# Half of the MLP up-projections of two stages as pairs of 64-row matmuls in two row halves of the array

## The chip, the cores and the metric

One NeuronCore of a Trainium2 chip runs the whole program. The metric is the device time of one execution in microseconds. The kernel before was timed in three runs, and one execution of it was recorded by the profiler.

## The reference

Three transformer blocks follow one another on one sequence of 1024 tokens with 1024 features, all in float32. Each block has a mixer (gated delta rule and neighbourhood attention in the first, sliding-window attention and a convolution in the second, gated linear attention and a convolution in the third) and an MLP. The change touches only the MLPs of block 1 and block 3. In block 1 it is

```python
x = layer_norm(DEEPNORM_ALPHA * x + mix, ln1_g[l], ln1_b[l])
ff = jnp.square(jax.nn.relu(jnp.einsum('btd,df->btf', x, w1[l]) + b1[l]))
ff = jnp.einsum('btf,fd->btd', ff, w2[l]) + b2[l]
```

with 4096 hidden features. The MLP of block 3 is the same without the biases, after an RMS norm.

## The kernel before

**Data.** Activations are stored with features on the partitions and tokens along the free dimension. The 1024 tokens are two halves of 512. A float32 product is made of three matmuls on operands of type fp32r (a float32 rounded to fewer mantissa bits): each activation and each weight is split into a high and a low part, and the three passes are high by high, low activation by high weight and high activation by low weight (`passes`, L283).

**Units.** The work of TensorE is a list `order` of units. One unit uses 128x1024 weights, which SyncE loads into one of four slots (`load_sp`, L270). ScalarE makes `w_hi` (`split_act`, L275) and VectorE makes `w_lo` (`split_dve`, L280) two units ahead of use. The MLP of one half is 64 units: 32 of kind "up" and 32 of kind "down". An up unit makes 128 of the hidden features for 512 tokens: 8 contracted chunks of 128 rows by 3 passes, 24 matmuls of 128x512 into one PSUM bank (`unit_part`, L341). A down unit also has 24 matmuls, 12 into each of two banks (L319), and it contracts four hidden chunks.

**Order.** An MLP half runs five up units, then four down, four up, four down and so on in eight groups: the first up unit of the next group stands ahead of the down units of a group, so the four chunks that a group of down units reads are ready one unit early. Only in the last group do the down units come directly behind the last up unit.

**Eviction of an up unit.** ScalarE applies Relu from PSUM into `u_act` (L373), which frees the bank, squares it into `h_hi` (L375) and again in place (L376). VectorE subtracts to get `h_lo` (L386). A down unit is added to the residual by VectorE (L402), and so is a unit of kind "out", the output projection (L408). Background units use two pairs of banks in turn, so a unit needs the pair that the unit before the last one used.

**Order by hand.** All engines walk the same list of steps (`walk`). A step may carry pieces of other work ("segments"), and on each engine those come first, then the weight split for the unit two places on, then the unit's own eviction. Each engine's queue is strictly in order. In the first half of MLP 1, the layer norm of the other half is laid beside units 0, 2, 4, ... 14 (`ln_dve`: sum L549, centring L555, squares folded L484 to L496, scaling L510, `low` L567 and L569). In the second half of MLP 3 the final RMS norm of the first half is laid beside units 2 to 8 (L484 to L500, L510). In both stages no other background runs.

Of the kernel before, what the change touches and what calls it, by code (L numbers as in the profile page):

```python
# [10 lines left out]
ALU = mybir.AluOpType  # L11
ACT = mybir.ActivationFunctionType
AX = mybir.AxisListType

P = 128
D = 1024
DC = D // P
T = 1024
HALF = 512
TC = T // P  # L20
# [103 lines left out]
def build_program(nc, g):  # L124

    ctx = ExitStack()
    with ctx:
# [16 lines left out]
        def sem(name):  # L144
            return ctx.enter_context(nc.semaphore(name))

        def param(name, j=0, n=1):
            return params[:, bass.ds(j + PARAMS[name][0], n)]
# [29 lines left out]
        def acts(h, low, c, t0=META, t1=W):  # L178
            return acts1[:, low, c, t0 - META:t1 - META] if h else acts0[:, low, c, t0:t1]
# [10 lines left out]
        u_act = mlp.take("u_act", [P, 2, HALF])  # L190
        out_at = mlp.at

        ps = ctx.enter_context(nc.psum_tensor("ps", [P, 8, HALF], F32))
# [4 lines left out]
        def tokens(h, t=None):  # L198
            t = xT if t is None else t
            return t[:, :, h * HALF:(h + 1) * HALF]  # L200
# [24 lines left out]
                self.ks, self.back, self.whole, self.taken = range(DC), None, kind in WHOLE, 0  # L225


        early1, last_down = [], []
        WHOLE = ("ab1", "cv1", "z1", "nq1", "nk1")
        NV = 4  # L230
        order = []
# [22 lines left out]
        def unit_done(eng, u):  # L254
            if u.src is None:
                eng.wait_ge(side_done, u.side + 1)
            else:
                eng.wait_ge(mm_done[u.z], u.turn + 1)

        def bank_free(u):  # L260
            return free[u.pool][u.slot]

        def own_free(eng, u):
            eng.wait_ge(bank_free(u), u.use + 1)
# [18 lines left out]
        def passes(z):  # L283

            return (w_hi[z], 0), (w_hi[z], 1), (w_lo[z], 0)
# [40 lines left out]
        def unit_part(pe, u, first, stop):  # L326

            if first == 0 and u.taken:
                if u.use:
                    pe.wait_ge(bank_free(u), u.use)  # L330
                pe.wait_ge(w_split[u.z], u.turn + 1)
            for h in range(2) if u.whole else [u.half]:
                spans = [(0, W // 2), (W // 2, W)] if u.meta else [(META, W)]
                for i_k in range(first, stop):
                    k = u.ks[i_k]
                    if u.gate is not None:
                        u.gate(pe, h, i_k)
                    for i, (w, low) in enumerate(passes(u.z)):
                        for b, (t0, t1) in enumerate(spans):
                            bank = u.bank + (h if u.whole else b)  # L340
                            last = nc.tensor.matmul(ps[:, bank, 0:t1 - t0], w[:, k * P:(k + 1) * P], acts(h, low, k, t0, t1),  # L341
                                                    start=(i_k == 0 and i == 0), stop=(i_k == DC - 1 and i == 2))
            if stop == DC:
                last.then_inc(mm_done[u.z], 1)
# [11 lines left out]
        def unit_act(act, u):  # L356
            if u.kind in ("out", "down"):
                return
            if u.kind == "nv1":
                if u.j == NV - 1:  # L360
                    nv1_act(act)
                return
            if u.kind in EVICT_ACT:
                unit_done(act, u)
                EVICT_ACT[u.kind](act, u)
                return
            if u.kind == "up":
                s = u.chunk % 2
                unit_done(act, u)
                if u.chunk >= 2:  # L370
                    act.wait_ge(hid_ready, u.chunk - 1)
                bias = param("b1", 4 * u.gr + u.j) if u.bias else 0.0
                nc.scalar.activation(u_act[:, s, :], ps[:, u.bank, :], ACT.Relu, bias=bias).then_inc(bank_free(u), 1)  # L373
                own_free(act, u)
                nc.scalar.activation(h_hi[:, u.chunk % RING, :], u_act[:, s, :], ACT.Square)  # L375
                nc.scalar.activation(u_act[:, s, :], u_act[:, s, :], ACT.Square).then_inc(hid_hi, 1)  # L376

        def unit_dve(dve, u):
            if u.kind == "nv1" and u.j == NV - 1:
                nv1_dve(dve)  # L380
            if u.kind in EVICT_DVE:
                EVICT_DVE[u.kind](dve, u)
            if u.kind == "up":
                r = u.chunk % RING
                dve.wait_ge(hid_hi, u.chunk + 1)
                nc.vector.tensor_tensor(h_lo[:, r, :], u_act[:, u.chunk % 2, :], h_hi[:, r, :].bitcast(F32), ALU.subtract)\  # L386
                    .then_inc(hid_ready, 1)
            if u in last_down:
                for c in range(2):
                    if c:  # L390
                        unit_done(dve, u)
                    else:
                        dve.wait_ge(tail_tile, 1)
                    one = tokens(u.half)[:, 2 * u.j + c, :]
                    nc.vector.tensor_tensor(one, one, ps[:, u.bank + c, :], ALU.add).then_inc(bank_free(u) if c else tail_added, 1)
                    if c == 0:
                        last_fold_dve(dve, rms_final[1])
                return
            if u.kind == "down":
                unit_done(dve, u)  # L400
                two = tokens(u.half)[:, 2 * u.j:2 * u.j + 2, :]
                nc.vector.tensor_tensor(two, two, ps[:, u.bank:u.bank + 2, :], ALU.add).then_inc(bank_free(u), 1)  # L402
            if u.kind == "out":
                unit_done(dve, u)
                if u.back is not None:
                    dve.wait_ge(u.back, 48)
                one = xT[:, u.j, u.half * HALF:(u.half + 1) * HALF]
                nc.vector.tensor_tensor(one, one, ps[:, u.bank, :], ALU.add).then_inc(bank_free(u), 1)  # L408
# [272 lines left out]
        def last_fold_dve(dve, m):  # L681
            m.wait(dve, "pre", 2)
            nc.vector.tensor_tensor(m.q[:, 0, :], m.q[:, 0, :], m.q[:, 1, :], ALU.add).then_inc(m.s["pre"], 1)
# [149 lines left out]
        def nv1_act(act):  # L833
            for at, b in enumerate(NV_LAST):
                if at < TC - 1:
                    act.wait_ge(nv_pe, at + 1)
                else:
                    unit_done(act, nv1s[-1])
                nc.scalar.activation(n_v[:, b, :], ps[:, b, :], ACT.Copy).then_inc(nv_act, 1)
                if at == 4:  # L840
                    for d in range(2):
                        identity_act(act, d)

        def nv1_dve(dve):
            for d in range(2):
                decayed_dve(dve, 0, d)
                for piece in first_level(dve, 0, d):
                    pass
# [345 lines left out]
        go = {name: sem(f"go_{name}") for name in ["sq", "sum", "ln", "rs", "norm", "end"]}  # L1194
# [1376 lines left out]
        gl = {name: old for name, (old, _) in zip(gl_names, gl_old)}  # L2571
        gl0 = {name: count for name, (_, count) in zip(gl_names, gl_old)}

        def gla_pool(pool):

            pool.wait_ge(sa["end"], sa0["end"] + 2 * HB)
            pool.wait_ge(c_tap, 2 * CC * CK)
            nc.gpsimd.dma_start(metaT[:, :, :], g["meta"]).then_inc(l_in, 16)
            nc.gpsimd.dma_start(l_wg[:, :], g["w_gate"]).then_inc(l_in, 16)
            nc.gpsimd.dma_start(l_mask[:, :, :], g["gla_consts"]).then_inc(l_in, 16)  # L2580
# [575 lines left out]
        mlp1 = [mlp_half("w_mlp1", h, True) for h in range(2)]  # L3156
        mlp2 = [mlp_half("w_mlp2", h) for h in range(2)]
        mlp3 = [mlp_half("w_mlp3", h) for h in range(2)]
# [135 lines left out]
        one = [(u, ()) for u in proj1]  # L3294
# [19 lines left out]
        last = [(u, ()) for u in mlp3[1]]  # L3314
# [7 lines left out]
        for m in (mlp1, mlp2, mlp3):  # L3322
            for h in range(2):
                chunk0 = m[h][0].chunk
                for u in m[h]:
                    if u.kind == "down":
                        u.first = chunk0 + 4 * u.gr
        early1.extend(proj1[:2])
        FIRST1 = len(proj1)
        AHEAD = 2  # L3330

# [23 lines left out]
        def _(sp):  # L3355
# [13 lines left out]
            for u in proj1:  # L3369
                if u.n + SLOTS < FIRST1:  # L3370
                    load_sp(sp, order[u.n + SLOTS])
# [12 lines left out]
            sp.wait_ge(na["av"], NP * ROWS)  # L3384
            for u in order[FIRST1:FIRST1 + SLOTS]:
                if u.z == 0:
# [3 lines left out]
            residual_sp(sp, 1)  # L3390
            for u in order[FIRST1 + SLOTS:]:
                load_sp(sp, u)
# [18 lines left out]
        def _(act):  # L3411
            act.preload_act_table_set(LOG_EXP)
            front_act(act)
            walk(act, front, "act", unit_act, split_act, 0, FIRST1)
            end1_act(act)
            walk(act, rest, "act", unit_act, split_act, FIRST1)

        @block.vector
        def _(dve):
# [3 lines left out]
            front_dve(dve)  # L3423
            walk(dve, front, "dve", unit_dve, split_dve, 0, FIRST1)
            end1_dve(dve)
# [146 lines left out]
```

## Time and profile before

| | us |
|---|---|
| three timed runs | 3663.24 median (3659.82 to 3664.07) |
| the profiled execution, its own time | 3661.55 |
| span of its trace | 3659.4 |
| TensorE matmuls busy | 3598.4 (98%) |
| VectorE busy | 2144.2 (59%) |
| ScalarE busy | 1579.6 (43%) |
| granted clock of TensorE, mean share of full speed | 0.995 |

The profiled execution took 2.2 us more than its span, which is what lies outside the first and the last instruction. The two stages that the change touches are the first half of MLP 1 (784.7 to 1135.2 us of the span) and the second half of MLP 3 (3298.1 to 3646.7 us), and TensorE is busy all through both of them.

### The profile page before, as it was taken

To read this page: it belongs to the slowest core of one execution; us is meant where nothing else is said; L and a number is where in the kernel's file an instruction comes from. 1 tells how busy PE (TensorE), PEld (TensorE's weight loads), DVE (VectorE), ACT (ScalarE), POOL (GpSimd) and SP (SyncE) were. 2 spreads that over 40 slices of the span, in tenths; PEclk is the share of its full clock that TensorE was granted. 3 is DMA by queue.
4 is the path that set the end of the run, shared out by engine and by line. 5 is a ranking of instruction groups with operands and counts; after the bars stand their busy time and mean duration, and the time that the engine had idled before them with its cause. 6 is when DMAs were issued, how large, how long until landed. Compare 5 with 4: busy or idle time off the path is not lost.

```text
span 3659.4 us, 50653 instructions
## 1 busy us (share of the span) xinstructions
PE 3598.4 (98%) x21121; PEld 2959.4 (81%) x21121; DVE 2144.2 (59%) x3262; ACT 1579.6 (43%) x2544; POOL 81.4 (2%) x85
## 2 busy tenths in 40 slices
PE   8999899999999999999999999999999999999998
PEld 5888778788888878888888889888888888888887
DVE  5741687775345578757588564366655266555333
ACT  5451666644334444535344452333443333434333
POOL 0000121000000000000000000000000000000000
PEclk9999899999999999999999999999999999999999
DMA  5124321324322222222222322222222222223222
GB/s 202 47 72 113 78 68 51 119 92 115 106 97 98 96 84 78 96 97 93 90 78 93 98 88 91 93 81 87 86 94 97 93 87 81 84 95 121 98 98 87
DMA packets 118891, 340.27 MB, mean 93 GB/s; under 512 B 20089, under 2 KB 32393, under 8 KB 118537
## 3 DMA queue, kind: packets, MB, share of 16 engines
q1 hardware_dynamic: 116424, 331.52, 28.0%
q0 software_dynamic: 2240, 5.51, 0.7%
q8 instruction: 169, 2.77, 0.3%
q14 instruction: 58, 0.47, 0.0%
HBM read 318.47 MB, written 20.06 MB: 93 GB/s over the span
## 4 chain that ended last, share of the span: by engine, by line
PE 94%; DVE 4%; ACT 1%; issue 1%; DMA 0%; SPq 0%; ACTq 0%; DVEq 0%
PE ps L341 54%; PE ps L319 28%; PE ps L1337 1%; PE ps L821 1%; PE ps L2847 1%; PE ps L1045 1%; PE ps L1693 1%; PE ps L1660 1%; DVE n_s L1782 1%; PE ps L1348 1%; PE ps L2276 0%; DVE g_D L1524 0%; PE ps L2303 0%; PE ps L1670 0%; PE ps L1380 0%
## 5 line engine op out<-in xcount | busy, mean ns | idle before, releaser
L341 PE MATMUL ps<-acts,w_hi 128*128 128x512 f32 (+1 forms) x6064 | 1813.1, 383 | 2.5 <-ACT l_vf L2683 0.8
L341 PEld LDWEIGHTS ps<-acts,w_hi 128*128 128x128 f32 x6064 | 1110.2, 188 | 231.9 <-issue 10.6
L341 PE MATMUL ps<-acts,w_lo 128*128 128x512 f32 (+1 forms) x3032 | 1136.1, 381 | 0.0
L280 DVE TENSOR_TENSOR w_lo<-w_raw,w_hi 128x1024 fp32r<-128x1024 f32 x539 | 657.8, 1221 | 390.9 <-ACT w_hi L275 387.9
L275 ACT ACTIVATE w_hi<-w_raw 128x1024 fp32r<-128x1024 f32 x539 | 563.6, 1050 | 500.3 <-DMA w_raw<-in_w_mlp 316.5
L341 PEld LDWEIGHTS ps<-acts,w_lo 128*128 128x128 f32 x3032 | 561.5, 188 | 110.0
L319 PE MATMUL ps<-h_hi,w_hi 128*128 128x512 f32 x1528 | 478.0, 394 | 0.0
L319 PE MATMUL ps<-h_lo,w_hi 128*128 128x512 f32 x1528 | 471.1, 390 | 0.0
L319 PE MATMUL ps<-h_hi,w_lo 128*128 128x512 f32 x1528 | 470.9, 389 | 0.0
L386 DVE TENSOR_TENSOR h_lo<-u_act,h_hi 128x512 fp32r<-128x512 f32 x192 | 132.8, 692 | 436.4 <-ACT u_act L376 435.9
L402 DVE TENSOR_TENSOR xT<-xT,ps 128x1024 f32<-128x1024 f32 x191 | 232.8, 1219 | 235.1 <-PE ps L319 234.4
L319 PEld LDWEIGHTS ps<-h_hi,w_lo 128*128 128x128 f32 x1528 | 286.8, 188 | 60.4
L319 PEld LDWEIGHTS ps<-h_lo,w_hi 128*128 128x128 f32 x1528 | 286.8, 188 | 60.3
L319 PEld LDWEIGHTS ps<-h_hi,w_hi 128*128 128x128 f32 x1528 | 283.6, 188 | 62.3 <-issue 4.4
L373 ACT ACTIVATE u_act<-ps 128x512 f32<-128x512 f32 x128 | 76.4, 596 | 336.6 <-PE ps L341 336.6
L2247 DVE SCALAR_TENSOR_TENSOR mixh<-c_pad,params,mixh 128x512 f32<-128x512 f32 x240 | 163.6, 744 | 0.0
L373 ACT ACTIVATE u_act<-ps,params 128x512 f32<-128x512 f32 x64 | 44.0, 688 | 191.1 <-PE ps L341 191.1
L375 ACT ACTIVATE h_hi<-u_act 128x512 fp32r<-128x512 f32 x192 | 121.4, 632 | 6.1
L376 ACT ACTIVATE u_act<-u_act 128x512 f32<-128x512 f32 x192 | 118.2, 616 | 0.0
L408 DVE TENSOR_TENSOR xT<-xT,ps 128x512 f32<-128x512 f32 x48 | 32.9, 686 | 123.8 <-PE ps L341 123.8
L2909 ACT ACTIVATE l_e<-l_e 128x256 f32<-128x256 f32 x56 | 23.4, 418 | 139.9 <-DVE l_e L2945 138.9
L476 ACT ACTIVATE acts<-mixh 128x512 fp32r<-128x512 f32 x64 | 40.5, 633 | 78.3 <-DVE mixh L510 77.2
(392 smaller groups left out, 2944.0 us busy)
## 6 DMA issues: line engine op xcount, KB each, us to landing
w_raw<-in_w_mlp SPq DMA_DIRECT2D x384, 512.0 KB, 3.4
w_raw<-in_w_in SPq DMA_DIRECT2D x107, 512.0 KB, 3.4
w_raw<-in_w_out SPq DMA_DIRECT2D x48, 512.0 KB, 3.4
n_bias<-na_tab SPq DMA_DIRECT2D x36, 256.0 KB, 4.6
xT<-in_x SPq DMA_DIRECT2D x8, 512.0 KB, 8.2
x<-xT SPq DMA_DIRECT2D x2, 2048.0 KB, 8.2
g_row<-gate_rows SPq DMA_DIRECT2D x16, 256.0 KB, 3.4
xT<-x SPq DMA_DIRECT2D x2, 2048.0 KB, 12.4
```

Of the source, the lines that this page charges most:

```text
L275: nc.scalar.activation(w_hi[u.z][:, :], w_raw[u.z][:, :], ACT.Copy).then_inc(w_hi_done[u.z], 1)
L280: nc.vector.tensor_tensor(w_lo[u.z][:, :], w_raw[u.z][:, :], w_hi[u.z][:, :].bitcast(F32), ALU.subtract).then_inc(w_split[u.z], 1)
L319: last = nc.tensor.matmul(ps[:, u.bank + c, :], w[:, k * 256 + c * P:k * 256 + (c + 1) * P], act[:, (u.first + k) % RING, :], start=(k == ...
L341: last = nc.tensor.matmul(ps[:, bank, 0:t1 - t0], w[:, k * P:(k + 1) * P], acts(h, low, k, t0, t1), start=(i_k == 0 and i == 0), stop=(i_k ...
L373: nc.scalar.activation(u_act[:, s, :], ps[:, u.bank, :], ACT.Relu, bias=bias).then_inc(bank_free(u), 1)
L375: nc.scalar.activation(h_hi[:, u.chunk % RING, :], u_act[:, s, :], ACT.Square)
L376: nc.scalar.activation(u_act[:, s, :], u_act[:, s, :], ACT.Square).then_inc(hid_hi, 1)
L386: nc.vector.tensor_tensor(h_lo[:, r, :], u_act[:, u.chunk % 2, :], h_hi[:, r, :].bitcast(F32), ALU.subtract)\
L402: nc.vector.tensor_tensor(two, two, ps[:, u.bank:u.bank + 2, :], ALU.add).then_inc(bank_free(u), 1)
L476: nc.scalar.activation(acts(m.half, 0, c), src, ACT.Copy).then_inc(m.s["hi"], 1)
L821: last = nc.tensor.matmul(ps[:, b, :], acts(b // HB, low, 2 * u.j + k, t0, t0 + P), w[:, k * HALF:(k + 1) * HALF], start=(u.j == 0 and k = ...
L2247: nc.vector.scalar_tensor_tensor(y, x, w, y, op0=ALU.mult, op1=ALU.add).then_inc(c_tap, 1)
```

## The change

The 64 up units of these two half-MLPs form the list `by_rows`. Each of their 24 matmuls of 128 contracted rows becomes two of 64 rows: partitions 0 to 63 go to one half of the array's rows and accumulate into bank `u.bank`, partitions 64 to 127 go to the other half and accumulate into `u.bank + 1`. The two banks must then be added. ScalarE copies the second bank into `u_act`, VectorE adds the first bank onto it and frees both, ScalarE applies Relu with the bias in place, waits for its own write, and goes on with the two squares as before. `rows_copied` and `rows_relu` are semaphores of an earlier stage, counted on from there.

```diff
@@ unit_part @@
                     for i, (w, low) in enumerate(passes(u.z)):
+                        if u in by_rows:
+                            for b in range(2):
+                                rows = slice(P // 2 * b, P // 2 * b + P // 2)
+                                last = nc.tensor.matmul(ps[:, u.bank + b, :], w[rows, k * P:(k + 1) * P], acts(h, low, k)[rows],
+                                                        start=(i_k == 0 and i == 0), stop=(i_k == DC - 1 and i == 2))
+                            continue
@@ unit_act @@
-                nc.scalar.activation(u_act[:, s, :], ps[:, u.bank, :], ACT.Relu, bias=bias).then_inc(bank_free(u), 1)
-                own_free(act, u)
+                if u in by_rows:
+                    n = by_rows.index(u)
+                    nc.scalar.activation(u_act[:, s, :], ps[:, u.bank + 1, :], ACT.Copy).then_inc(rows_copied, 1)
+                    own_free(act, u)
+                    nc.scalar.activation(u_act[:, s, :], u_act[:, s, :], ACT.Relu, bias=bias).then_inc(rows_relu, 1)
+                    act.wait_ge(rows_relu, TC + n + 1)
+                else:
+                    nc.scalar.activation(u_act[:, s, :], ps[:, u.bank, :], ACT.Relu, bias=bias).then_inc(bank_free(u), 1)
+                    own_free(act, u)
@@ unit_dve @@
+            if u in by_rows:
+                dve.wait_ge(rows_copied, TC + by_rows.index(u) + 1)
+                one = u_act[:, u.chunk % 2, :]
+                nc.vector.tensor_tensor(one, one, ps[:, u.bank, :], ALU.add).then_inc(bank_free(u), 1)
             if u.kind == "up":
@@ after the units are placed @@
+        by_rows.extend(u for u in mlp1[0] + mlp3[1] if u.kind == "up")
```

## Rows read from the trace of the kernel before

**Rows 1.** The page: span, busy time of the engines, and the chain by engine.

```profile
span 3659.4 us, 50653 instructions
PE 3598.4 (98%) x21121; PEld 2959.4 (81%) x21121; DVE 2144.2 (59%) x3262; ACT 1579.6 (43%) x2544; POOL 81.4 (2%) x85
...
PE 94%; DVE 4%; ACT 1%; issue 1%; DMA 0%; SPq 0%; ACTq 0%; DVEq 0%
```

**Rows 2.** Windows over the two stages: length, busy us of each engine, clock, DMA.

```profile
784.70:1135.19 350.49, 350.49 (x1544) 288.87 (x1543) 170.25 (x172) 133.58 (x173) 9.21 (x16) 1.00 0.35 104
3298.06:3646.68 348.62, 348.62 (x1540) 288.67 (x1539) 151.45 (x148) 129.90 (x171) 4.34 (x8) 1.00 0.30 98
```

**Rows 3.** Timeline of PE: first matmuls of four up units and of those behind.

```profile
3478.04 0.61 PE L341 MATMUL ps<-acts,w_hi 128*128 128x512 f32 x2
...
3499.80 0.61 PE L319 MATMUL ps<-h_hi,w_hi 128*128 128x512 f32 x2
```

**Rows 4.** PE: pairs of 64-row matmuls, full float32 ones; then one group (busy, mean).

```profile
1341.38 0.61 PE L319 MATMUL ps<-h_hi,w_lo 128*128 128x512 f32 x2
1341.92 2.00 PE L2303 MATMUL ps<-s_k,s_q 64*128 64x256 f32 x16
1343.85 0.74 PE L319 MATMUL ps<-h_hi,w_hi 128*128 128x512 f32 x2
...
1344.90 0.40 PE L319 MATMUL ps<-h_hi,w_lo 128*128 128x512 f32 x1
...
2420.25 1.13 PE L2864 MATMUL ps<-l_vt,l_ket 128*128 128x256 f32 x4
...
L1045 PE MATMUL ps<-norm_b,consts 128*128 128x512 f32 x22 | 9.9, 597 | 2.4 <-ACT norm_b L1095 2.4
```

**Rows 5.** Timeline, one up unit's eviction and the matmuls that follow it.

```profile
3586.84 0.61 PE L319 MATMUL ps<-h_hi,w_hi 128*128 128x512 f32 x2
...
3587.03 0.60 ACT L373 ACTIVATE u_act<-ps 128x512 f32<-128x512 f32 x1 [2.71 <-PE ps L341]
...
3587.66 0.63 ACT L375 ACTIVATE h_hi<-u_act 128x512 fp32r<-128x512 f32 x1
...
3588.20 0.62 ACT L376 ACTIVATE u_act<-u_act 128x512 f32<-128x512 f32 x1
...
3588.72 1.04 ACT L275 ACTIVATE w_hi<-w_raw 128x1024 fp32r<-128x1024 f32 x1
3588.85 0.69 DVE L386 TENSOR_TENSOR h_lo<-u_act,h_hi 128x512 fp32r<-128x512 f32 x1 [3.27 <-ACT u_act L376]
```

**Rows 6.** Timeline of DVE and ACT at the start of MLP 1's first half.

```profile
789.27 0.69 DVE L408 TENSOR_TENSOR xT<-xT,ps 128x512 f32<-128x512 f32 x1
790.06 2.29 DVE L549 TENSOR_TENSOR mixh<-xT 128x2048 f32<-128x2048 f32 x1
790.23 0.69 ACT L373 ACTIVATE u_act<-ps,params 128x512 f32<-128x512 f32 x1 [6.35 <-PE ps L341]
...
795.39 0.69 DVE L386 TENSOR_TENSOR h_lo<-u_act,h_hi 128x512 fp32r<-128x512 f32 x1
...
798.30 4.48 DVE L555 SCALAR_TENSOR_TENSOR xT<-ps,xT 128x2048 f32<-128x2048 f32 x2
802.70 1.22 DVE L280 TENSOR_TENSOR w_lo<-w_raw,w_hi 128x1024 fp32r<-128x1024 f32 x1
```

**Rows 7.** Timeline of DVE at units 12 to 14 of that stage.

```profile
854.06 2.73 DVE L510 SCALAR_TENSOR_TENSOR xT<-xT,params,mixh 128x512 f32<-128x512 f32 x4
...
860.95 1.22 DVE L280 TENSOR_TENSOR w_lo<-w_raw,w_hi 128x1024 fp32r<-128x1024 f32 x1
```

**Rows 8.** Timeline of DVE and PE around unit 4 of MLP 3's second half.

```profile
3317.01 2.42 DVE L484 TENSOR_TENSOR mixh<-mixh 128x1024 f32<-128x1024 f32 x2
...
3323.90 0.69 DVE L496 TENSOR_TENSOR mixh_r<-mixh 128x512 fp32r<-128x512 f32 x1
...
3325.26 0.39 PE L499 MATMUL ps<-mixh_r,ones_r 128*128 128x512 f32 x1
```

More of the change, by code:

```diff
@@ L225, in __init__ @@
                 self.ks, self.back, self.whole, self.taken = range(DC), None, kind in WHOLE, 0
-        early1, last_down = [], []
+        early1, last_down, by_rows = [], [], []
         WHOLE = ("ab1", "cv1", "z1", "nq1", "nk1")
@@ L2572, in build_program @@
         gl0 = {name: count for name, (_, count) in zip(gl_names, gl_old)}
+        rows_copied, rows_relu = go["sq"], go["sum"]
         def gla_pool(pool):
```

## The prediction

> **What bounds the kernel now.** I read the page first. It shows TensorE busy for 98% of the span, and 94% of the chain that ends last is TensorE's [rows 1]. Then I read the windows over the two stages that the change touches: in both, TensorE's busy time equals the window, 350.49 of 350.49 us and 348.62 of 348.62 us, while VectorE is busy for 170.25 and 151.45 us and ScalarE for 133.58 and 129.90 us, at a granted clock of 1.00 throughout [rows 2]. So here any change of the matmuls' pace and any wait of TensorE goes straight into the time. VectorE and ScalarE have room on average, but an average hides their short crowded stretches, and the chain they form is lengthened by this change, so I read the timeline there.
>
> **The pace of the matmuls.** Four up units have 96 matmuls and take 3499.80 - 3478.04 = 21.76 us, so 0.2267 us for each and 5.44 us for a unit [rows 3]. After the change a unit has 24 pairs. What does a pair cost? The kernel before has pairs of 64 rows in both row halves and different banks, but in plain float32. Full float32 matmuls of 512 columns take 9.9/22 = 0.45 us each, so some 0.22 for 256 columns. Four of 128x256 take 1.13 us together, sixteen records of 64x256, which are eight pairs, take 2.00 [rows 4]. If the 64-row ones had to take turns, sixteen would need 1.13 + 12 x 0.22 = 3.8 us. If two run at once, eight pairs need 1.13 + 4 x 0.22 = 2.01 us, and 2.00 is what the row shows. So a float32 pair costs what one full float32 matmul costs, (2.00 - 1.13)/4 = 0.2175 us.
>
> No row shows a 64-row matmul of fp32r, which streams 512 columns in 0.2267 us where float32 needs about 0.2175 for 256. The lower bound for a pair is the float32 pair's, 0.215 with the rounding of its rows; the upper is two matmuls in turn, 0.453 us. I take 0.2267, because the halves behave as two independent streams in rows 4 and each stream has the pace of rows 3. The 64 units have 64 x 24 = 1536 pairs, so the change of pace is 0 by this choice, 1536 x (0.215 - 0.2267) = -18.0 us at the lower end and 1536 x 0.2267 = +348 us at the upper.
>
> The Trainium skill puts a price on each further tile: TensorE: Matmul & The Clock Gate, "Measured speedup vs the span model", has a span of one matmul plus about 4 ns for every tile more. If that were paid in every pair, an estimate from its figure is 1536 x 4 ns = 6 us more. Rows 4 speak for its being paid once in a run of pairs, since eight pairs fit in 2.00 us without it.
>
> **The change of the array's shape.** In rows 4 the full matmuls at 1341.38 and those at 1344.90 are 3.52 us apart. Between these starts lie six full matmuls, 6 x 0.2267 = 1.36 us, and eight pairs, 8 x 0.2175 = 1.74 us, which makes 3.10. The switch to 64 rows and back costs the other 0.42 us: about 0.28 as gaps around the block and 0.14 as matmuls that start too slowly after it. Up units stand in eight runs in each half, and the sums of the layer norm after unit 1 cut one run of MLP 1, so there are 17 round trips, 17 x 0.42 = 7.1 us. Where TensorE is going to wait for VectorE anyway (below) they cost nothing, so I count about 6.3 us.
>
> **The eviction, where nothing else runs.** Let E be the end of an up unit, that is the start of the next matmul, 3586.84. Before, Relu starts at E + 0.19, frees the bank at E + 0.79, and VectorE starts `h_lo` at E + 2.01 and ends at E + 2.70 [rows 5]. After: copy 0.60, the add 0.69 (the row of L408, also 512 columns from PSUM [rows 6]), Relu in SBUF 0.62 (as L376), the squares 0.53 to the second's start and 0.62, `h_lo` 0.69, and 0.03 at each of four crossings [rows 5]. That is 3.87 us, so `h_lo` ends at E + 4.06 and the banks are free at E + 1.5. The unit that needs the banks starts at E + 5.44, so nothing waits. The last chunk of a group is needed 18 matmuls into the down units, 4.08 us after they start, and normally one up unit lies between: slack 5 us. In the last group none does. There the weights of that matmul would load at about E + 3.85, so TensorE waits some 0.3 us, twice: 0.5 us.
>
> The new adds are 64 x 0.69 = 44 us of VectorE and the new Relus 64 x 0.62 us of ScalarE. In quiet stretches this lies beside TensorE. But both engines are in order, and each now waits for the other inside each unit: ScalarE stands after its copy until VectorE reaches the add, and behind ScalarE stand the weight splits, for which VectorE waits next.
>
> **The eviction beside the layer norm of MLP 1.** Here I followed the three queues with the durations of the rows. Before, unit 0's Relu starts at 790.23, but VectorE is in the norm's sums and reaches its `h_lo` only at 795.39 [rows 6]; that was harmless, since ScalarE had freed the bank and gone on. After, the add is first there: 795.4 to 796.1. Relu and squares end at 798.0, then comes ScalarE's split for unit 3 (till 799.0), VectorE's split (till 800.2), the add of unit 1 (800.8), Relu, squares and `h_lo` (till 803.3), then the two centring operations of 4.4 us (807.7), the split for unit 4 (808.9) and the add of unit 2, which frees unit 4's banks at 809.5. TensorE wants unit 4 at 807.0: a wait of 2.5 us, and 0.2 us at unit 2. Units 6 to 8 have the folding of the squares on VectorE (2.42 us for L484's two [rows 8], 1.22 and three times 0.69, so 5.7 us) in the same way, and the add of unit 6 ends at 833.8 where TensorE would start unit 8 at 831.6: 2.6 us with what is lost before unit 6.
>
> At units 10 to 14 the norm gives VectorE four scalings (2.73 us [rows 7]) at unit 10, four scalings and four `low` steps (854.06 to 860.95, 6.9 us [rows 7]) at unit 12, and four more `low` steps at unit 14. Before, the split for unit 14 runs from 860.95 to 862.17 [rows 7], and unit 14 starts in that moment: there is no slack. After, units 10 and 11 each pass through split, add, Relu, squares and `h_lo` one behind another, about 4.7 us each, so `h_lo` of unit 11 starts at 861.7 where the add of its own bank could have been free at 857. Then 2.65 + 4.24 + 1.2 us bring the split for unit 14 to 870.4, and TensorE, itself moved by the waits so far, would start at 866.5: a wait of about 4.5 us, with 0.8 more at unit 16. From unit 17 on nothing waits. The sum for MLP 1 is 0.2 + 2.5 + 2.6 + 4.5 + 0.8 = 10.6 us.
>
> **The eviction beside the final norm of MLP 3.** Before, the last folded sum is done at 3323.90 + 0.69 = 3324.59, and TensorE's sum matmuls come at 3325.26, between units 4 and 5 [rows 8]: a slack of 0.7 us. After, `h_lo` of unit 2 ends at 3319.3 in place of 3317.0, the fold waits for the second square, which stands on ScalarE behind unit 2 (till 3320.5), so the fold ends near 3323.0, the split for unit 5 at 3324.2, the add of unit 3 at 3324.8, its Relu, squares and `h_lo` at 3327.2, and the three operations up to L496 at 3329.3. TensorE waits 4.1 us.
>
> **The sum.** Pace 0, switches +6.3, waits of MLP 1 +10.6, of MLP 3 +4.1, ends of the halves +0.5: +21.5 us. The profiled execution took 3661.6 us, and the median of the runs is 1.6 above it, so 3683 for such an execution and 3684 for the median (rounded down by a few tenths). The waits can be off by some 4 us either way, since one operation in another order moves them.
>
> **Rivals.**
> (1) The pair runs at the float32 pair's 0.2175. For it: the shape of the array is the same. Against: whatever makes an fp32r matmul 0.009 us longer than a float32 one of half its columns is there in each half too. The pace gives back 14 us, but where TensorE comes sooner it waits longer, so following the queues again leaves +9 us: 3672.
> (2) The fp32r halves take turns, so the change does not do what it says. For it: no fp32r pair is in the trace. Against: the float32 pairs. The waits vanish, since a unit then has 10.9 us: 348 + 7.1 = +355, so 4018.
> (3) The engines absorb the longer eviction, say because VectorE's steps overlap more than I take, and only the switches and ends are left: +7.6, so 3671. Against: VectorE has next to no idle time in these stretches [rows 6 to 8].
> (4) The small offset between the tiles is paid in each pair. With 7 ns, 1536 x 7 = 10.8 us: 3694.
> (5) The other sign: the pace pays for all else. At 0.215 it gives back 18.0 us against 7.1 for the switches. To be faster by more than 0.2% (7.3 us, about what a measurement of this kernel can tell from no change) needs 18.0 - 7.1 - waits > 7.3, so it decides when all waits together stay under 3.6 us. Then about 3654.
>
> **Chances and range.** The forecast has 0.58, (1) 0.10, (2) 0.11, (3) 0.12, (4) 0.06, (5) 0.03. The range 3668 to 3706 holds the forecast with its spread, (1), (3) and (4), and leaves (2) and (5) out. Cases (1) and (3) lie at the border of 3670.6, so I give half of their 0.22 to "same": faster 0.03, same 0.11, slower 0.86.
>
> **What would show it.** Right: the starts of pairs 0.227 us apart in an up run; about 0.2 us more at each change between up and down; TensorE idle for 2 to 5 us before units 4, 8 and 14 of MLP 1 and before the sum matmuls near 3325 in MLP 3, ended by VectorE; no idle time in the quiet groups; `h_lo` ending about 4.1 us after an up unit. Wrong: a pace of pairs other than 0.227, which weighs most at 1.5 us for each ns; or VectorE's queue drifting by other amounts at units 10 to 14.

## The result, and the profile after

The kernel with the change takes 3688.0 us in the median (3685.3 to 3689.9), the one before 3663.65 us in runs on the same chip: +24.4 us, a ratio of 1.0064 [1.0050, 1.0077]. The forecast was 3684 us with a range of 3668 to 3706 us, and slower with 0.86. The profiled execution took 3689.05 us for a span of 3687.0 us, and the lines of its page that answer to [rows 1] are these:

```profile
span 3687.0 us, 53853 instructions
PE 3618.9 (98%) x22657; PEld 2967.4 (80%) x22657; DVE 2187.4 (59%) x3326; ACT 1618.6 (44%) x2608; POOL 81.4 (2%) x85
...
PE 91%; DVE 6%; ACT 2%; issue 1%; DMA 0%; ACTq 0%; SPq 0%; DVEq 0%
...
L342 PE MATMUL ps<-acts,w_hi 64*128 64x512 f32 x2048 | 317.9, 389 | 1.6 <-DVE u_act L399 1.6
...
L342 PE MATMUL ps<-acts,w_lo 64*128 64x512 f32 x1024 | 199.7, 387 | 0.0
```

The 3072 matmuls of 64 rows are there, so TensorE has 1536 matmuls more than before. VectorE works 43 us more and ScalarE 39 us more, of the 44 and 40 us forecast. TensorE's part of the chain fell from 94% to 91% and VectorE's rose from 4% to 6%: that is the first sign that much of the time went into waits for VectorE. The windows say how much. The first two rows are the two changed stages and answer to [rows 2]; the others are stretches inside them, which are used below. The columns are length, busy time of TensorE, its weight loads, VectorE, ScalarE and GpSimd, then TensorE's clock.

```profile
790.41:1154.23 363.82, 357.07 (x2312) 288.56 (x2311) 191.31 (x204) 152.25 (x205) 9.22 (x16) 1.00 0.35 100
3315.36:3674.28 358.92, 354.83 (x2307) 289.39 (x2307) 173.06 (x180) 149.06 (x203) 4.33 (x8) 0.99 0.31 96
877.75:895.62 17.87, 17.87 (x72) 14.41 (x73) 12.95 (x16) 6.73 (x9) 1.85 (x3) 0.92 0.43 84
895.62:917.63 22.01, 22.01 (x194) 17.95 (x193) 10.03 (x11) 10.73 (x16) 1.79 (x3) 1.00 0.59 130
3347.99:3371.66 23.67, 23.67 (x97) 19.13 (x95) 14.95 (x18) 8.06 (x10) 4.33 (x8) 0.92 0.44 156
...
3393.67:3415.68 22.01, 22.01 (x100) 17.95 (x98) 9.73 (x10) 7.46 (x9) 0.00 (x0) 1.00 0.31 96
```

MLP 1 takes 363.82 us in place of 350.49, so 13.3 us more, and MLP 3 358.92 in place of 348.62, so 10.3 us more. TensorE is no longer busy for the whole of either: 6.75 and 4.09 us are idle. The two stages make 23.6 us. The profiled executions differ by 27.6 us, and the other 4.0 us lie outside them: MLP 1 starts 5.7 us later, the stretch between the stages is 1.7 us shorter, and what follows is the same 12.72 us. In front of MLP 1 nothing was changed; there the clock's mean from 400 us to the stage is 0.96 in this execution and 0.98 in that of before, with the same matmuls. I take the 5.7 us for a difference between executions, since the medians differ by 24.4 us, close to the 23.6 of the stages. No run separates it.

The waits of TensorE in those stages, three in MLP 1 and one in MLP 3, in us with their count and longest:

```profile
PE ps L319 <- DVE u_act L399: 3.6, 1, 3.6
PE ps L342 <- DVE u_act L399: 1.6, 1, 1.6
PE ps L319 <- DVE xT L419: 1.5, 1, 1.5
...
PE ps L516 <- DVE mixh_r L513: 4.1, 1, 4.1
```

L399 is the new add. And TensorE's timeline at the four places, at the third two small matmuls of another stage, L2141, stand in front (start, us from first to last end, then the idle time before in brackets):

```profile
813.39 0.39 PE L342 MATMUL ps<-acts,w_lo 64*128 64x512 f32 x2
815.40 0.73 PE L342 MATMUL ps<-acts,w_hi 64*128 64x512 f32 x4 [1.62 <-DVE u_act L399]
...
838.03 0.39 PE L517 MATMUL ps<-mixh_r,ones_r 128*128 128x512 f32 x1
839.95 0.74 PE L319 MATMUL ps<-h_hi,w_hi 128*128 128x512 f32 x2 [1.54 <-DVE xT L419]
...
873.35 0.81 PE L2141 MATMUL ps<-s_t,s_rel 32*8 32x384 f32 x2
877.75 1.22 PE L319 MATMUL ps<-h_hi,w_hi 128*128 128x512 f32 x2 [3.58 <-DVE u_act L399]
...
3342.49 0.39 PE L342 MATMUL ps<-acts,w_lo 64*128 64x512 f32 x2
3346.97 0.79 PE L516 MATMUL ps<-mixh_r,ones_r 128*128 128x512 f32 x1 [4.09 <-DVE mixh_r L513]
```

They are units 4, 8 and 14 of MLP 1 and the sum matmuls of MLP 3, the places that the forecast named. There is no other wait in the two stages.

Why VectorE is late at unit 4 is seen in its queue and ScalarE's at that time:

```profile
801.12 0.68 DVE L399 TENSOR_TENSOR u_act<-u_act,ps 128x512 f32<-128x512 f32 x1
803.77 0.69 DVE L403 TENSOR_TENSOR h_lo<-u_act,h_hi 128x512 fp32r<-128x512 f32 x1 [1.97 <-ACT u_act L389]
...
809.13 4.48 DVE L572 SCALAR_TENSOR_TENSOR xT<-ps,xT 128x2048 f32<-128x2048 f32 x2
813.53 1.22 DVE L280 TENSOR_TENSOR w_lo<-w_raw,w_hi 128x1024 fp32r<-128x1024 f32 x1
814.66 0.68 DVE L399 TENSOR_TENSOR u_act<-u_act,ps 128x512 f32<-128x512 f32 x1
```

```profile
809.34 0.58 ACT L381 ACTIVATE u_act<-ps 128x512 f32<-128x512 f32 x1
815.38 0.72 ACT L383 ACTIVATE u_act<-u_act,params 128x512 f32<-128x512 f32 x1 [5.46 <-DVE u_act L399]
```

VectorE idles 1.97 us inside a unit, between its add and `h_lo`, while ScalarE does Relu and the squares: that is what the crossing between the engines costs. Then the centring of the layer norm (4.48 us for its two) and the weight split stand in front of the add that frees the bank, so ScalarE's copy, done at 809.92, stays without an answer until 815.34, and TensorE starts at 815.40. Each engine waits for the other by turns, and TensorE for both.

### The profile page after: what moved, and what is told of

Its sections match the earlier page's. It is cut to its first block, busy times and chain, and to the rows that moved or that the text cites. A ratio compares the mean times of both kernels' runs of the same rounds, so it can differ in the third digit from the quotient of the medians.

```text
span 3687.0 us, 53853 instructions
## 1 busy us (share of the span) xinstructions
PE 3618.9 (98%) x22657; PEld 2967.4 (80%) x22657; DVE 2187.4 (59%) x3326; ACT 1618.6 (44%) x2608; POOL 81.4 (2%) x85
## 4 chain that ended last, share of the span: by engine, by line
PE 91%; DVE 6%; ACT 2%; issue 1%; DMA 0%; ACTq 0%; SPq 0%; DVEq 0%
PE ps L347 44%; PE ps L319 27%; PE ps L342 8%; PE ps L1354 2%; PE ps L838 1%; PE ps L2866 1%; PE ps L1062 1%; PE ps L1710 1%; DVE w_lo L280 1%; PE ps L1677 1%; PE ps L1365 1%; PE ps L2293 0%; DVE n_s L1799 0%; PE ps L2320 0%; PE ps L1687 0%
## 5 line engine op out<-in xcount | busy, mean ns | idle before, releaser
L347 PE MATMUL ps<-acts,w_hi 128*128 128x512 f32 (+1 forms) x5040 | 1496.9, 382 | 2.5 <-ACT l_vf L2702 0.8
L347 PEld LDWEIGHTS ps<-acts,w_hi 128*128 128x128 f32 x5040 | 917.7, 188 | 190.8 <-issue 10.1
L347 PE MATMUL ps<-acts,w_lo 128*128 128x512 f32 (+1 forms) x2520 | 937.2, 380 | 0.0
L347 PEld LDWEIGHTS ps<-acts,w_lo 128*128 128x128 f32 x2520 | 465.1, 188 | 89.8
L342 PE MATMUL ps<-acts,w_hi 64*128 64x512 f32 x2048 | 317.9, 389 | 1.6 <-DVE u_act L399 1.6
L342 PEld LDWEIGHTS ps<-acts,w_hi 64*128 64x128 f32 x2048 | 191.0, 184 | 47.2 <-issue 5.6
L342 PE MATMUL ps<-acts,w_lo 64*128 64x512 f32 x1024 | 199.7, 387 | 0.0
L386 ACT ACTIVATE u_act<-ps 128x512 f32<-128x512 f32 x96 | 57.2, 596 | 224.3 <-PE ps L347 224.3
L342 PEld LDWEIGHTS ps<-acts,w_lo 64*128 64x128 f32 x1024 | 96.0, 184 | 20.4
```

The lines of the kernel that those rows point to most:

```text
L342: last = nc.tensor.matmul(ps[:, u.bank + b, :], w[rows, k * P:(k + 1) * P], acts(h, low, k)[rows], start=(i_k == 0 and i == 0), stop=(i_k ...
```

## The experiments

The first four kernels shared a chip and runs of the kernel before (median 3664.7 us, 21 runs), the other four as well (3663.5 us, 9 runs). Differences are against those.

**Which half of the change costs?** One kernel (`e1_eviction_alone`) keeps the new eviction and gives each of the two banks four of the eight chunks with all 128 rows; so there are the old matmuls and no pairs:

```
-    for b in range(2):
-        rows = slice(P // 2 * b, P // 2 * b + P // 2)
-        last = nc.tensor.matmul(ps[:, u.bank + b, :], w[rows, ...], acts(h, low, k)[rows], ...)
+    b = i_k // (DC // 2)
+    last = nc.tensor.matmul(ps[:, u.bank + b, :], w[:, ...], acts(h, low, k),
+                            start=(i_k % (DC // 2) == 0 and i == 0), ...)
```

> The 64 up units keep full 128-row matmuls, but chunks 0 to 3 go to the first bank and 4 to 7 to the second, with the eviction of the changed kernel (copy, add, Relu, two squares). No switch of the array's shape. My theory (long eviction beside the norms makes TensorE wait): about +15 us, with waits before units 4, 8, 14 of MLP 1 and before the sums of MLP 3, plus 2 to 4 us if the granted clock falls after a wait. Rival (the pairs and their switches cost it all): within 2 us of the kernel before.

It took 3679.7 us, a ratio of 1.0042 [1.0029, 1.0055], +15.0 us. The other kernel (`e2_pairs_alone`) keeps the pairs and evicts only the first bank, as before, so what is in the second bank is left out of the result:

```
-                if u in by_rows:
+                if False:
     (in unit_act, and the same in unit_dve)
```

> Pairs of 64-row matmuls as in the changed kernel, but the eviction of the kernel before: Relu reads the first bank alone, so the upper 64 rows' share is left out of the result. My theory: pairs keep 0.227 us, no waits, 17 round trips of the array's shape at 0.45 to 0.5 us: +8 us. Rival (pairs are slower than full matmuls): more than +12 us. Rival (all comes from the eviction): 0.

It took 3671.6 us, 1.0019 [1.0010, 1.0028], +6.9 us. The waits of the first in the two stages, and the windows over the two stages of the second:

```profile
PE ps L319 <- DVE u_act L398: 3.8, 1, 3.8
PE ps L341 <- DVE u_act L398: 2.2, 1, 2.2
PE ps L319 <- DVE xT L418: 1.5, 1, 1.5
...
PE ps L515 <- DVE mixh_r L512: 4.1, 1, 4.1
```

```profile
785.06:1139.78 354.72, 354.72 (x2312) 287.58 (x2311) 170.26 (x172) 133.56 (x173) 9.21 (x16) 1.00 0.36 103
3302.80:3655.27 352.47, 352.47 (x2308) 287.33 (x2307) 151.26 (x148) 129.87 (x171) 4.33 (x8) 1.00 0.31 98
```

With the eviction alone all four waits stay, though TensorE does the old matmuls. With the pairs alone TensorE is busy for the whole of both windows, the clock is at its full level, and they still take 4.2 and 3.9 us more than [rows 2]. The two parts make 21.9 us of the 24.4; the other 2.5 us are within the intervals of these medians. The eviction costs more than twice what the pairs do.

**Where do they cost?** One kernel has the change from unit 17 of MLP 1 and unit 9 of MLP 3 on, which is 50 of the 64 up units and 13 of the 17 round trips, where no norm runs beside the units; the other has it for the 14 units ahead of these:

```
-        by_rows.extend(u for u in mlp1[0] + mlp3[1] if u.kind == "up")
+        by_rows.extend(u for u in mlp1[0][17:] + mlp3[1][9:] if u.kind == "up")   (quiet units)
+        by_rows.extend(u for u in mlp1[0][:17] + mlp3[1][:9] if u.kind == "up")   (busy units)
```

> Pairs and long eviction only in the 50 up units that have no norm beside them (from unit 17 of MLP 1 and from unit 9 of MLP 3). My theory: no waits but the small ones at the two ends, 13 round trips of 0.49 us: +6 to +7 us. Rival (the long eviction costs everywhere, 25 us over 64 units): 50/64 of it, about +19 us.

> The opposite of the quiet units: pairs and long eviction only in the 14 up units beside the norms (first 9 of MLP 1, first 5 of MLP 3). My theory: all the waits are here, 14 to 15 us, plus some 2 us for four round trips partly under the waits, plus 2 to 4 us if the clock falls: +15 to +19 us. Rival (cost in proportion to units): 14/64 of 25, about +5 us.

The quiet units took 3669.3 us, 1.0013 [1.0005, 1.0022], +4.6 us, and no wait. By its interval this median is uncertain by some 3 us. The two stages of the profiled execution leave out what varies elsewhere, and they are 3.2 and 3.5 us longer than [rows 2]:

```profile
788.29:1141.96 353.67, 353.67 (x2095) 287.78 (x2094) 186.06 (x196) 147.62 (x196) 9.21 (x16) 1.00 0.36 103
3302.98:3655.11 352.13, 352.13 (x2188) 287.36 (x2187) 169.91 (x175) 146.48 (x198) 4.33 (x8) 1.00 0.31 98
```

The busy ones took 3680.0 us, 1.0043 [1.0030, 1.0055], +15.3 us, with waits of 3.6, 1.6, 1.5 and 4.1 us, the same four as in the changed kernel. So 50 of the 64 units cost no more than what changing the array's shape costs, with the whole longer eviction hidden, and the other 14 pay for the waits. What is beside those 14, and not beside the 50, is the work of a norm: a layer norm in MLP 1, the final RMS norm in MLP 3.

**Is it the order of VectorE's queue?** The add of a unit stands behind the weight split of a later one. This kernel puts it ahead of that split:

```
+        def add_rows(dve, u):
+            dve.wait_ge(rows_copied, TC + by_rows.index(u) + 1)
+            one = u_act[:, u.chunk % 2, :]
+            nc.vector.tensor_tensor(one, one, ps[:, u.bank, :], ALU.add).then_inc(bank_free(u), 1)
...
-            if u in by_rows:
-                ... (the same three lines in unit_dve)
+                if split is split_dve and u in by_rows:
+                    add_rows(eng, u)
```

> The changed kernel with one thing moved: on VectorE the add of an up unit stands before the weight split for the unit two places on, not behind it. The work is the same. My theory (the cost is the order of VectorE's queue and ScalarE standing behind it): following the queues again gives 5.8 us less waiting in MLP 1 and 1.7 less in MLP 3, so about +14 us against the kernel before in place of +21, and the wait before unit 4 of MLP 1 shrinks from 2.5 to 0.8 us. Rival (the cost is the amount of added work on the engines): no change against the changed kernel, +24 us.

It took 3678.3 us, 1.0036 [1.0022, 1.0049], +14.9 us: 9.5 us of the 24.4 were the place of one instruction. In the two stages the waits at units 4 and 8 of MLP 1 are gone, and the two that are left are about half of what they were:

```profile
PE ps L319 <- DVE w_lo L280: 2.1, 1, 2.1
...
PE ps L517 <- DVE mixh_r L514: 2.3, 1, 2.3
```

The stages take 359.06 and 354.94 us, 8.6 and 6.3 us above before. The wait at unit 14 is now for the split itself: whichever of add and split stands second is late, since neither order makes VectorE's work there less.

**Is each change of shape a cost?** Every second up unit of the quiet stretches as pairs (26 of them in place of 50) halves the pairs and doubles the changes, to 26 round trips in place of 13:

```
+        for us in (mlp1[0][17:], mlp3[1][9:]):
+            by_rows.extend([u for i, u in enumerate(us) if u.kind == "up" and i % 2 == 0])
```

> Only every second up unit of the quiet 50, so 26 units in pairs and 26 round trips of the array's shape in place of 13. My theory (cost per switch): twice the quiet run's switch cost, about +12 us and the ends. Rival (cost per pair): half of the quiet run's, +2 to +3 us.

It took 3675.0 us, 1.0033 [1.0021, 1.0046], +11.5 us, with half as many pairs as the quiet units' kernel, that took +4.6. The stages say it more sharply than the medians do; TensorE waits in neither:

```profile
788.75:1145.33 356.58, 356.58 (x1832) 286.94 (x1830) 178.75 (x185) 141.18 (x185) 9.24 (x16) 1.00 0.35 102
3307.98:3663.51 355.53, 355.53 (x1876) 286.38 (x1875) 161.06 (x162) 138.87 (x185) 4.36 (x8) 1.00 0.30 97
```

They are 6.1 and 6.9 us longer than [rows 2], 13.0 us for 26 round trips, where the quiet units have 6.7 us for 13: 0.50 and 0.51 us for a round trip. By the medians it is 11.5/26 = 0.44 and 4.6/13 = 0.35 us. A cost per pair is out; the cost goes with the changes.

**Do the halves run at once, and what if they could not?** Here both matmuls of a pair take rows 0 to 63, and the other 64 rows of the contraction are left out:

```
-                                rows = slice(P // 2 * b, P // 2 * b + P // 2)
+                                rows = slice(0, P // 2)
```

> Both matmuls of a pair read partitions 0 to 63, so both go to the same half of the array's rows; the lower 64 rows are counted twice and the upper ones left out. If two halves of the array are what makes the pair cost one matmul, the pair now takes 0.453 us and the time rises by about 348 + 8 = 356 us. Rival (the second matmul of a pair is cheap whatever rows it uses, since half of the array is idle): as the changed kernel.

One run took 4019.5 us, +356 us. Its timeline has six matmuls in 1.36 us where the changed kernel has six in 0.68:

```profile
819.66 1.07 PE L342 MATMUL ps<-acts,w_hi 64*128 64x512 f32 x4
820.57 0.61 PE L342 MATMUL ps<-acts,w_lo 64*128 64x512 f32 x2
821.02 1.07 PE L342 MATMUL ps<-acts,w_hi 64*128 64x512 f32 x4
```

```profile
901.22 0.62 PE L342 MATMUL ps<-acts,w_hi 64*128 64x512 f32 x4
901.67 0.39 PE L342 MATMUL ps<-acts,w_lo 64*128 64x512 f32 x2
901.89 0.39 PE L342 MATMUL ps<-acts,w_hi 64*128 64x512 f32 x2
```

Two matmuls of one half cost 0.453 us and two of different halves 0.227 us. This is rival (2)'s time, to 2 us of its 4018, so the second matmul of a pair is free only when it takes the other 64 rows. The two here also read the same partitions of the activations and weights; no run separates that from the half of the array.

**Does the order of a pair's matmuls matter?** In this kernel the three matmuls of a chunk for rows 0 to 63 stand in the program ahead of all three for rows 64 to 127 (the recorded expectation calls these the lower and the upper half):

```
-                    for i, (w, low) in enumerate(passes(u.z)):
-                        if u in by_rows:
-                            for b in range(2):
+                    if u in by_rows:
+                        for b in range(2):
+                            for i, (w, low) in enumerate(passes(u.z)):
```

> Same work as the changed kernel, but the three passes of the lower half are issued before the three of the upper half. If TensorE starts matmuls in program order, the second and third pass of a half wait for the one before, and only the seams overlap: four steps of 0.227 us for each chunk in place of three, so 64 x 8 x 0.227 = +116 us on top of the changed kernel, less what waits vanish: about 3780 us. Rival (the halves run on their own whatever the order): as the changed kernel.

One run took 3684.6 us, no slower than the changed kernel. My expectation was wrong: with starts in program order it would have been about 3780 us. The timeline is in the changed kernel's rhythm, six matmuls in 0.68 us:

```profile
900.02 0.62 PE L342 MATMUL ps<-acts,w_hi 64*128 64x512 f32 x4
900.47 0.40 PE L342 MATMUL ps<-acts,w_lo 64*128 64x512 f32 x2
900.70 0.62 PE L342 MATMUL ps<-acts,w_hi 64*128 64x512 f32 x4
```

The single records inside these groups start at 900.020 and 900.030, 900.247 and 900.257, 900.473 and 900.483 us, two by two, in the changed kernel 3 to 4 ns apart. In program order the weights are w_hi, w_hi, w_lo for one half and then the same for the other; the records have four with w_hi and then two with w_lo. So the first matmul of rows 64 to 127 starts 10 ns behind the first of rows 0 to 63, and not behind their third, which stands ahead of it in the program.

## Why the prediction was right

**The pace of a pair** was taken as one fp32r matmul's, 0.2267 us [rows 3], not the float32 pair's 0.2175. Right: in the rows above a chunk's three pairs take 0.68 us, and rival (1), with its 14 us back, has no row. Nothing is paid per pair either, which ends rival (4): the second matmul's 3 to 4 ns overlap with the next pair. A pace that gives nothing back ends rival (5). The Trainium skill's model (TensorE: Matmul & The Clock Gate, "Measured speedup vs the span model"), which would have made 6 us if paid each time, agrees with the offset of this trace, but the offset does not add up over a run of pairs. The 7 ns of rival (4) are the offset in the trace's float32 pairs of [rows 4]; these pairs have 3 to 4.

**The change of shape** was 0.42 us a round trip, from one float32 block [rows 4]. An up run takes 22.01 us and the down run behind it 22.01 us, in place of 21.76 each [rows 3]: 0.25 us at either end, 0.50 together. So the term was right in kind and small in size: 17 x 0.50 = 8.5 us, and 8.1 us in the windows of the pairs alone, where 7.1 was forecast and 6.3 counted. The Trainium skill says that a change of the tiling mode drains TensorE (TensorEngine Tiling (Array Packing), "Key Properties"). It gives no price; the trace agrees that there is one, 0.25 us for each change.

**The eviction in quiet stretches** was forecast to end `h_lo` 4.06 us after the unit. The up unit that starts at 895.62 ends where the next unit's first pair starts, at 901.22 (a line of the timeline of pairs above), and VectorE does this for it:

```profile
902.05 0.69 DVE L399 TENSOR_TENSOR u_act<-u_act,ps 128x512 f32<-128x512 f32 x1 [3.97 <-ACT u_act L381]
904.71 0.69 DVE L403 TENSOR_TENSOR h_lo<-u_act,h_hi 128x512 fp32r<-128x512 f32 x1 [1.98 <-ACT u_act L389]
```

So `h_lo` ends at 905.40, 4.18 us after. The 0.12 us more are mostly the Relu in SBUF, 0.72 us in the rows above where 0.62 was taken. Nothing waits for it, as the quiet units' kernel shows. The 0.5 us at the ends of the halves did not appear: there is no such wait in either stage.

**The waits of MLP 1** were at the right units, through the right queues, and each was forecast too large. From start to start, less one matmul, TensorE loses 2.01 - 0.23 = 1.8 us at unit 4 (2.5 forecast) and 1.92 - 0.23 = 1.7 at unit 8 (2.6). At unit 14 the two starts are 4.40 us apart, 0.74 before, so 3.7 us (4.5). There is no wait for the 0.2 and 0.8 us of units 2 and 16. That is 7.2 us of 10.6. VectorE's steps follow each other more closely than I let them: the split at 813.53 starts 0.08 us before the 4.48 us of the centring are over.

**The wait of MLP 3** was 4.1 us, and is 4.09.

**Not forecast: the clock.** The waits of about 4 us are followed by a stretch at the lower level (below), which costs 1.4 us in MLP 1 and 2.4 in MLP 3. With it the sums close. MLP 1: 7.2 for waits, 9 x 0.50 for shapes, 1.4 for the clock, which makes 13.1 and was measured as 13.3. MLP 3: 4.1 + 8 x 0.50 + 2.4 = 10.5, measured 10.3; one of its changes lies partly inside the wait. So that the forecast total of 21.5 us came so near 24.4 was in part luck: 3.4 us too much wait and 0.5 for the ends stood against 3.8 us of clock and 8.5 - 6.3 = 2.2 of shape left out.

**Of the rivals**, (3) holds for the 50 quiet units and not for the 14 beside the norms. (2) is what happens with both matmuls in one half.

## What to carry to other kernels

Splitting a contraction of 128 rows over two row halves bought TensorE nothing here (fp32r, 512 columns), as a pair takes as long as the matmul that it replaces, and it costs twice: at each change of the array's shape, and by an eviction that now has to join two banks across two engines. A busy share of 59% on the engine that joins them says little; look in the timeline for the stretches where something else already fills it, follow the queues there by hand, and put what frees a bank ahead of what is only due later.

## What was not expected of the hardware

The granted clock is at the full level (2.4 GHz) through both stages before. After, it falls to 1.2 GHz in the two long waits, those of 3.58 and 4.09 us, and stays there for a while behind them:

```profile
877.20:880.60 3.40, 2.85 (x7) 2.27 (x8) 1.19 (x2) 2.84 (x5) 0.00 (x0) 0.50 0.00 0
3345.00:3351.80 6.80, 4.83 (x11) 3.80 (x12) 4.27 (x6) 3.62 (x8) 0.00 (x0) 0.50 0.13 51
```

TensorE works for 2.85 and 4.83 us of these windows, at half the pace, which costs 1.4 and 2.4 us; of the 2.4, 1.9 are in the four units that take 23.67 us in place of 21.76, the rest in the two sum matmuls ahead of them. In the timeline the first matmuls behind the wait at 877.75 take 1.22 us for two, against 0.74 at 839.95 behind the wait of 1.54 us. The eviction alone has the falls too, with a longer one in MLP 1: the three units behind its wait of 3.8 us take 18.80 us, against 17.87 here and 72 x 0.2267 = 16.32 at the full level, so nearly the same wait was followed by a loss of 1.5 us in one execution and of 2.5 in the other. In the kernel with the add ahead of the split the clock does not fall in MLP 3, where the wait is 2.3 us, but does behind the 2.1 us in MLP 1:

```profile
866.36 0.81 PE L2142 MATMUL ps<-s_t,s_rel 32*8 32x384 f32 x2
869.25 0.70 PE L319 MATMUL ps<-h_hi,w_hi 128*128 128x512 f32 x2 [2.09 <-DVE w_lo L280]
...
870.33 1.05 PE L319 MATMUL ps<-h_hi,w_lo 128*128 128x512 f32 x2
871.19 1.05 PE L319 MATMUL ps<-h_hi,w_hi 128*128 128x512 f32 x2
...
873.67 0.62 PE L319 MATMUL ps<-h_hi,w_hi 128*128 128x512 f32 x2
```

Two matmuls start 0.85 us apart there and 0.45 at the full level. The kernels with no wait in the stages, the pairs alone and the quiet units, have no fall there. The fall behind the 2.1 us comes only after TensorE has started again, and the three units there take 18.12 us, so it costs 1.8 us. A wait in these dense stages thus cost between nothing and 0.9 of its length again. In MLP 1 TensorE had run two small matmuls (32 rows, 8 columns of weights) just before the wait, in MLP 3 the pairs of an up unit; no run separates this from the rest, and what decides between 2.1 us with a fall and 2.3 us without stays open.

The two row halves start their matmuls each for itself, as far as one run shows it. The Trainium skill has matmuls start strictly in program order (TensorE: Matmul & The Clock Gate, "The mechanism"). The kernel with three matmuls of a half ahead of the other's three shows them starting 10 ns apart, which that rule excludes; here the measurement decides.
